# Norm sums by 32 columns of ones in four column groups, and norm roots held as rows of 128 tokens

## The reference

```python
def sandwich(x, mod, g_pre, g_post, fn):                 # first block: four times
    shift, scale, gate = mod
    h = rms_norm(x, g_pre) * (1.0 + scale[:, None]) + shift[:, None]
    return x + gate[:, None] * rms_norm(fn(h), g_post)

for i in range(DEPTH):                                   # second block: two layers
    m = hybrid_mixer(...) if i % 2 == 0 else mla_mixer(...)
    h = layer_norm(DN_ALPHA * x + m, ln1_g[i], ln1_b[i])
    f = jnp.square(jax.nn.relu(h @ mlp_w1[i])) @ mlp_w2[i]
    e = jax.nn.sigmoid(h @ ple_w_gate[i]) * (p[i] @ ple_w_proj[i])
    x = layer_norm(DN_ALPHA * h + f + e, ln2_g[i], ln2_b[i])
```

## Time and profile before

| | |
|---|---|
| median of three runs | 2917.77 us (2916.14 to 2920.08) |
| the profiled execution, whole time | 2916.7 us |
| its span from first to last instruction | 2914.9 us |
| PE, share of the span | 96% |
| PEld, share of the span | 80% |
| DVE, share of the span | 41% |
| POOL, share of the span | 32% |
| ACT, share of the span | 31% |

### The profile page before, as it was taken

One profiled execution on the slowest core, in us unless ns is written; L12 is line 12 of the kernel. 1 busy time (PEld: TensorE's weight loads), 2 busy tenths in 40 slices (PEclk: granted clock), 3 DMA queues, 4 the chain that ended last, 5 costly groups with the idle time before them and its releaser, 6 DMA issues.

```text
span 2914.9 us, 35811 instructions
## 1 busy us (share of the span) xinstructions
PE 2802.8 (96%) x14000; PEld 2325.7 (80%) x14000; DVE 1192.6 (41%) x1913; ACT 909.4 (31%) x1240; POOL 923.8 (32%) x223
## 2 busy tenths in 40 slices
PE   8998999999999999999999899999998999999998
PEld 7787888888778777888886787888887778788887
DVE  6666354053522234101248723614423561361532
ACT  3343322222333233222233524212223542421222
POOL 1220234433322222434333114444432111444431
PEclk9999999999999999999999999999999999999999
DMA  7430444343222211232222012222221111222221
GB/s 283 182 116 1 157 151 152 142 175 109 80 63 77 65 44 67 89 104 101 78 89 73 30 37 101 86 101 101 87 80 36 52 44 37 101 101 93 95 101 44
DMA packets 44457, 271.36 MB, mean 93 GB/s; under 512 B 5119, under 2 KB 8727, under 8 KB 16440
## 3 DMA queue, kind: packets, MB, share of 16 engines
q1 hardware_dynamic: 40320, 266.23, 25.6%
q10 hardware_dynamic: 4024, 3.54, 0.5%
HBM read 267.62 MB, written 2.13 MB: 93 GB/s over the span
## 4 chain that ended last, share of the span: by engine, by line
PE 66%; issue 25%; POOL 5%; DVE 3%; ACT 1%; POOLq 0%; DVEq 0%; ACTq 0%
PE lin L685 18%; PE lin L687 18%; PE lin L686 18%; POOL wlo L650 5%; PE bank L810 2%; PE bank L1115 1%; PE lin L1095 1%; PE bank L1107 1%; ACT whi L1556 1%; PE bank L1266 0%; PE bank L1383 0%; DVE dqr L2514 0%; PE bank L1247 0%; PE bank L1082 0%; PE bank L827 0%
## 5 line engine op out<-in xcount | busy, mean ns | idle before, releaser
L650 POOL TENSOR_TENSOR wlo<-raw,whi 128x2048 fp32r<-128x2048 f32 (+3 forms) x215 | 923.4, 4295 | 1950.4 <-ACT whi L1556 1950.4
L685 PE MATMUL lin<-hhi,whi 128*128 128x512 f32 x1976 | 786.2, 398 | 18.8 <-POOL wlo L650 8.6
L687 PE MATMUL lin<-hhi,wlo 128*128 128x512 f32 x1976 | 774.6, 392 | 0.0
L686 PE MATMUL lin<-hlo,whi 128*128 128x512 f32 x1976 | 774.5, 392 | 0.0
L1556 ACT ACTIVATE whi<-raw 128x2048 fp32r<-128x2048 f32 (+3 forms) x215 | 384.7, 1789 | 994.9 <-PE lin L687 955.5
L685 PEld LDWEIGHTS lin<-hhi,whi 128*128 128x128 f32 x1976 | 374.3, 189 | 110.1 <-issue 19.8
L685 PE MATMUL lin<-ghi,whi 128*128 128x512 f32 x1120 | 441.2, 394 | 0.8 <-issue 0.8
L687 PEld LDWEIGHTS lin<-hhi,wlo 128*128 128x128 f32 x1976 | 374.0, 189 | 79.7
L687 PE MATMUL lin<-ghi,wlo 128*128 128x512 f32 x1120 | 436.2, 389 | 0.0
L686 PE MATMUL lin<-glo,whi 128*128 128x512 f32 x1120 | 436.0, 389 | 0.0
L686 PEld LDWEIGHTS lin<-hlo,whi 128*128 128x128 f32 x1976 | 374.7, 190 | 76.3 <-issue 1.2
(11 more groups left out here) (407 smaller groups left out, 2807.2 us busy)
## 6 DMA issues: line engine op xcount, KB each, us to landing
raw<-in_w SPq DMA_DIRECT2D x169, 1024.0 KB, 4.9
adw_a<-in_ada SPq DMA_DIRECT2D x30, 1024.0 KB, 4.9
adw_b<-in_ada SPq DMA_DIRECT2D x18, 1024.0 KB, 5.0
raw<-in_w SPq DMA_DIRECT2D x20, 768.0 KB, 4.3
raw<-in_w SPq DMA_DIRECT2D x16, 640.0 KB, 3.8
raw<-in_w SPq DMA_DIRECT2D x10, 512.0 KB, 3.5
x<-in_x SPq DMA_DIRECT2D x1, 2048.0 KB, 16.9
out<-x SPq DMA_DIRECT2D x8, 256.0 KB, 2.0
```

What stands on the lines that cost most here:

```text
L650: nc.gpsimd.tensor_tensor(wlo[:, slot, 0:size], raw[:, slot, 0:size], whi[:, slot, 0:size].bitcast(F32), ALU.subtract).then_inc(s.wlo_ok, 1)
L685: pe.matmul(dst, lh, rh, start=first, stop=False)
L686: pe.matmul(dst, lh, rl, start=False, stop=False)
L687: return pe.matmul(dst, ll, rh, start=False, stop=last)
```

## The change

The sums are turned over. The stationary operand becomes 32 columns of ones, the moving one the 128x128 piece of the squares, and the result goes to 32 partitions: group t of the tokens to partitions 32t to 32t+31 of the first 128 columns of the bank, each row the same 128 sums. The four matmuls of a chunk so use four column groups of the array. Root and reciprocal are taken of the whole 128x128 block (`r_rows`), in place of 128x4. The spread takes a broadcast column of the identity as the stationary operand, which picks row 32t, and the 128x128 rows as the moving one. Between the sums `keep_busy` runs twice in place of once in `norm_sums`, `ada_sums_first` and `mla_mixer`. The head norms of the first mixer keep `column_sums` and `spread`.

```diff
+        r_rows = sb("r_rows", [P, P])
+        mu_rows, ms_rows, k_rows = tmp[:, 1, 0:P], tmp[:, 1, P:2 * P], tmp[:, 1, 0:P]
...
+            def chunk_sums(bank, src, first, last):
+
+                for t in range(TT):
+                    mm = pe.matmul(bank[32 * t:32 * t + 32, 0:P], ones[:, 0:32], src[:, t * P:(t + 1) * P],
+                                   start=first, stop=last)
+                return mm
...
-                column_sums(B4, sq[:, k % 2, :], k == 0, k == DC - 1).then_inc(s.ss_mm, 1)
+                chunk_sums(B4, sq[:, k % 2, :], k == 0, k == DC - 1).then_inc(s.ss_mm, 1)
...
+            def spread_rows(bank, rows):
+
+                for t in range(TT):
+                    mm = pe.matmul(bank[:, t * P:(t + 1) * P], ident[:, 32 * t:32 * t + 1].broadcast_to([P, P]), rows,
+                                   start=(t == 0), stop=(t == TT - 1))
+                return mm
...
-                spread(B7, r4).then_inc(s.rr_mm, 1)
+                spread_rows(B7, r_rows[:, :]).then_inc(s.rr_mm, 1)
...
-                    keep_busy(1 if c < DC - 1 else 0)
+                    keep_busy(2 if c < DC - 1 else 0)
...
-                            keep_busy(1, LB[3])
+                            keep_busy(2, LB[3])
...
-                    column_sums(B5, m[:, k, :], k == 0, k == DC - 1)
-                    column_sums(B4, sq[:, k % 2, :], k == 0, k == DC - 1).then_inc(s.ss_mm, 1)
+                    chunk_sums(B5, m[:, k, :], k == 0, k == DC - 1)
+                    chunk_sums(B4, sq[:, k % 2, :], k == 0, k == DC - 1).then_inc(s.ss_mm, 1)
...
-                    keep_busy(1, LB[0])
+                    keep_busy(2, LB[0])
...
-                act.activation(r4, sums_of(B4), ACT.Sqrt, bias=eps, scale=scale).then_inc(s.rms_ok, 1)
+                act.activation(r_rows[:, :], B4[:, 0:P], ACT.Sqrt, bias=eps, scale=scale).then_inc(s.rms_ok, 1)
...
-                act.activation(mu4, sums_of(B5), ACT.Copy, scale=1.0 / D).then_inc(s.mu_ok, 1)
-                act.activation(ms4, sums_of(B5), ACT.Square, scale=1.0 / D).then_inc(s.act_to_dve, 1)
+                act.activation(mu_rows, B5[:, 0:P], ACT.Copy, scale=1.0 / D).then_inc(s.mu_ok, 1)
+                act.activation(ms_rows, B5[:, 0:P], ACT.Square, scale=1.0 / D).then_inc(s.act_to_dve, 1)
...
-                v.reciprocal(r4, r4).then_inc(s.rr_ok, 1)
+                v.reciprocal(r_rows[:, :], r_rows[:, :]).then_inc(s.rr_ok, 1)
```

More of the change, by code:

```diff
@@ L245, in program @@
         minus_spl = small[:, 16:20]
-        mu4, ms4, k4, spare = small[:, 48:52], small[:, 52:56], small[:, 56:60], small[:, 60:61]
+        spare = small[:, 60:61]
         mmax = small[:, 20:24]
@@ L1310, in layer_sums @@
                     pe.wait_ge(s.sq_ok, n.up(s.sq_ok))
-                    column_sums(B5, m[:, k, :], k == 0, k == DC - 1)
-                    column_sums(B4, sq[:, k % 2, :], k == 0, k == DC - 1).then_inc(s.ss_mm, 1)
+                    chunk_sums(B5, m[:, k, :], k == 0, k == DC - 1)
+                    chunk_sums(B4, sq[:, k % 2, :], k == 0, k == DC - 1).then_inc(s.ss_mm, 1)
             def layer_rows():
                 pe.wait_ge(s.mu_ok, n.up(s.mu_ok))
-                spread(B6, mu4)
+                spread_rows(B6, mu_rows)
                 root_rows(5)
@@ L1410, in mla_mixer @@
                     pe.wait_ge(s.sq_ok, n.up(s.sq_ok))
-                    column_sums(B4 if c < 4 else B5, sq[:, c % 2, :], c in (0, 4), c in (3, 5)).then_inc(s.ss_mm, 1)
+                    chunk_sums(B4 if c < 4 else B5, sq[:, c % 2, :], c in (0, 4), c in (3, 5)).then_inc(s.ss_mm, 1)
                     if c == 0:
@@ L1418, in mla_mixer @@
                 pe.wait_ge(s.rr_ok, n.up(s.rr_ok))
-                spread(B5, k4).then_inc(s.rr_mm, 1)
+                spread_rows(B5, k_rows).then_inc(s.rr_mm, 1)
                 keep_busy(4, LB[0])
@@ L1902, in z_squares @@
                 tile[0] += DC
-                act.activation(mu4, sums_of(B5), ACT.Copy, scale=1.0 / D).then_inc(s.mu_ok, 1)
-                act.activation(ms4, sums_of(B5), ACT.Square, scale=1.0 / D).then_inc(s.act_to_dve, 1)
+                act.activation(mu_rows, B5[:, 0:P], ACT.Copy, scale=1.0 / D).then_inc(s.mu_ok, 1)
+                act.activation(ms_rows, B5[:, 0:P], ACT.Square, scale=1.0 / D).then_inc(s.act_to_dve, 1)
                 act.wait_ge(s.dve_to_act, n.up(s.dve_to_act))
-                act.activation(r4, r4, ACT.Sqrt, bias=eps_ln).then_inc(s.rms_ok, 1)
+                act.activation(r_rows[:, :], r_rows[:, :], ACT.Sqrt, bias=eps_ln).then_inc(s.rms_ok, 1)
                 split_next()
@@ L2018, in mla_mixer @@
                 act.wait_ge(s.ss_mm, n.up(s.ss_mm, 2))
-                act.activation(r4, sums_of(B4), ACT.Sqrt, bias=eps_rms, scale=1.0 / 512).then_inc(s.rms_ok, 1)
-                act.activation(k4, sums_of(B5), ACT.Sqrt, bias=eps_rms, scale=1.0 / 256).then_inc(s.rms_ok, 1)
+                act.activation(r_rows[:, :], B4[:, 0:P], ACT.Sqrt, bias=eps_rms, scale=1.0 / 512).then_inc(s.rms_ok, 1)
+                act.activation(k_rows, B5[:, 0:P], ACT.Sqrt, bias=eps_rms, scale=1.0 / 256).then_inc(s.rms_ok, 1)
                 for c in range(6):
@@ L2582, in layer_norm @@
                 v.wait_ge(s.act_to_dve, n.up(s.act_to_dve))
-                v.scalar_tensor_tensor(r4, sums_of(B4), 1.0 / D, ms4, ALU.mult, ALU.subtract).then_inc(s.dve_to_act, 1)
+                v.scalar_tensor_tensor(r_rows[:, :], B4[:, 0:P], 1.0 / D, ms_rows, ALU.mult, ALU.subtract).then_inc(s.dve_to_act, 1)
                 recip()
@@ L2710, in mla_mixer @@
                 skip(7)
-                for cols in (r4, k4):
+                for cols in (r_rows[:, :], k_rows):
                     v.wait_ge(s.rms_ok, n.up(s.rms_ok))
```

## The result

The changed kernel takes 2883.86 us, median of four runs (2882.36 to 2887.24), against 2917.35 (2916.14 to 2920.08) for the kernel before on the same chip: a ratio of 0.9885, interval 0.987 to 0.9899. It is faster by 33.5 us; 24.6 were forecast. The profiled execution took 2882.36 us, of which 2880.6 are its span.

The account below looks back on a forecast made before the run. PE, busy 96% of the span, was taken as the bound. Projections -31.2 us and norm ends +6.6 sum to -24.6: 2892.1 from the profiled 2916.7, 2893 against the median; range 2875 to 2922, for full overlap 2875 to 2900.

Parts of the forecast that it names:

- The sum: Inside projections, one chunk's sum falls from 0.89 to 0.62 us and two in a row from 1.79 to 0.84.
- the switch: Going from whole-array to part-array matmuls and back, at each block of sums: 0.40 us, with 0 as other bound.
- The block of three: Three sums together behind the first unit of the second mixer's projection; the third waits for ACT's square: 0.3 us saved.
- ln1's ends: End of ln1's projection, twice: the last sum gives PE back 1.2 us earlier each, 2.4 for two.
- The reciprocal and the root: On each norm's path, 128x128 in place of 128x4: reciprocal 0.95 us, 0.78 more; root 0.37, 0.1 more.
- The ends of the norms: Longer root and reciprocal less 0.5 given back: +0.4 us per first-block projection end, +1.0 per `norm_sums` with its slower pace.
- the last mixer: The last mixer's norms: five paces of 0.15 us and two reciprocals, partly beneath `keep_busy`, 0.9 lost.
- ln2's ends: Ends of ln2, two: shorter last sums save 1.3 us, the longer chain through the reciprocal takes most back: -0.1 each.
- The first pre norm: First norm of the kernel: eight sums at 1.48 in place of 1.32 us and a later, longer reciprocal: 1.3 lost.
- (A): Rival: column groups don't overlap; a sum costs 1.26 us, a pair 2.12, the kernel 2971, +53; chance 0.14.
- (B): Rival: column groups overlap in twos; a sum costs 0.83 us, a pair 1.26, the kernel about 2920; chance 0.12.
- (C): Rival: PE's longer waits at twelve norms lower the clock, up to 1.5 us each, 2905 to 2911; chance 0.08.

## Why the prediction was right

The likeliest case, all four groups at once, is what happened, and 2883.9 lies in its own range (2875 to 2900). The gain was 33.5 where 24.6 were forecast, so the mechanism was right and several terms were mis-sized, nearly all to the same side. By the prediction's own steps:

**The sum** was predicted at 0.62 and a pair at 0.84. They take 0.56 and 0.77. The streaming term, 0.22 per sum, was right; the mis-sized term is the switch, 0.40 taken from matmuls on half the rows and 0.34 measured. The trace of the kernel before had no nearer row. The 21 single sums so save 0.33 each, 6.9 us (5.7 predicted), the 24 pairs 1.02 each, 24.5 (22.8).

**The block of three** was put at 0.3, because the third sum waits for ACT. It gave 1.05: before, the three cost 2.80 us (from 1083.53 on the trace of before, where the 24 records stand together), after, 1.75 (1081.76 to 1083.51):

```profile
1081.53 0.39 PE L689 MATMUL lin<-ghi,wlo 128*128 128x512 f32 x1
1081.85 0.64 PE L818 MATMUL bank<-sq,cst 128*32 128x128 f32 x16
1083.05 0.43 PE L818 MATMUL bank<-sq,cst 128*32 128x128 f32 x8 [0.56 <-ACT sq L1639]
1083.40 0.50 PE L687 MATMUL lin<-ghi,whi 128*128 128x512 f32 x1
```

The wait is real (0.56), but the square that ends it (it starts at 1082.40, released by PE's sums) needs a buffer that the first sums free, and they free it earlier. The step that failed took ACT's square as fixed in time.

**ln1's ends** were right: from the start of the last square to the product 2.60 before, and after from 1735.92 to 1737.18 + 0.11, 1.37:

```profile
1735.92 0.63 ACT L1916 ACTIVATE sq<-m 128x512 f32<-128x512 f32 x1 [5.65 <-DVE m L2587]
```

```profile
1736.60 0.43 PE L818 MATMUL bank<-m,cst 128*32 128x128 f32 x8 [0.91 <-ACT sq L1916]
...
1737.18 0.50 PE L687 MATMUL lin<-ghi,whi 128*128 128x512 f32 x1
```

Twice 1.23, 2.5 us (2.4 predicted). The projections together: 6.9 + 24.5 + 1.1 + 2.5 = 35.0 us, against 31.2.

**The reciprocal and the root** were right to the row: 953 ns (0.95) and 368 ns (0.37).

**The ends of the norms** were put too dear, since the shorter last sum gives back more than the 0.5 taken. In `norm_sums` the last sum starts 1.52 ahead of the reciprocal in the earlier trace rows and 0.96 ahead of it now, though the root between them is 0.11 longer: 0.67 given back. From the last sum to the spread it is 1.97 after 1.75. The pace is 1.42 (1.48 predicted, 1.39 in the earlier trace rows), and from the first sum to the last it is 9.92 after 9.75. That is 0.22 + 0.17 = 0.4 for each `norm_sums` where 1.0 was predicted, 1.2 for the three in place of 3.0. The pace was put too high by the same switch as above. The four projection ends cost 0.17 each in place of 0.4, the last mixer 0.3 in place of 0.9.

**ln2's ends** were put at -0.1 each, and the spread comes 0.8 earlier at each. Before:

```profile
2895.08 0.63 ACT L1900 ACTIVATE sq<-m 128x512 f32<-128x512 f32 x1 [12.05 <-DVE m L2575]
...
2898.65 0.18 DVE L2153 RECIPROCAL small<-small 128x4 f32<-128x4 f32 x1 [0.36 <-ACT small L1906]
...
2899.07 0.60 PE L817 MATMUL lin<-cst 128*128 128x256 f32 x2
...
2899.50 0.72 PE L827 MATMUL bank<-cst,small 128*128 128x128 f32 x5
```

After:

```profile
2861.43 0.63 ACT L1916 ACTIVATE sq<-m 128x512 f32<-128x512 f32 x1 [11.08 <-DVE m L2591]
...
2864.06 0.95 DVE L2169 RECIPROCAL r_rows<-r_rows 128x128 f32<-128x128 f32 x1 [0.47 <-ACT r_rows L1922]
2864.15 0.60 PE L826 MATMUL lin<-cst 128*128 128x256 f32 x2
...
2865.07 1.16 PE L843 MATMUL bank<-r_rows,cst 128*128 128x128 f32 x8 [0.33 <-DVE r_rows L2169]
```

Before, the reciprocal was done at 2898.83 and the spread started 0.67 later, behind PE's own `keep_busy`. The prediction summed the chain of mean, variance, root and reciprocal as if it were the path, and did not see that PE was the late one. Now PE waits for the reciprocal and the longer 0.95 sits mostly in that slack: from square to spread 3.64 in place of 4.42.

At the other ln2 it is 3.66 in place of 4.43, but there the spread itself is slow. Before and after:

```profile
2175.88 1.05 PE L827 MATMUL bank<-cst,small 128*128 128x128 f32 x8
```

```profile
2155.59 2.05 PE L843 MATMUL bank<-r_rows,cst 128*128 128x128 f32 x8
```

The granted clock is 1.00 from 2172 to 2181 us before, and 0.72 from 2153 to 2159 us after. So the 0.8 is lost again: from the last product ahead of the last sums to the first one behind the norm it is 11.38 us in place of 11.15. The two ends together give 0.6, not 1.6.

**The first pre norm** was put at +1.3. PE's first product starts at 53.85 in place of 50.83, +3.0. Here the first sums run at half pace, and `keep_busy` is dear there. After:

```profile
31.22 0.66 PE L818 MATMUL bank<-sq,cst 128*32 128x128 f32 x8
31.81 2.08 PE L826 MATMUL lin<-cst 128*128 128x256 f32 x4
...
37.44 1.13 PE L826 MATMUL lin<-cst 128*128 128x256 f32 x4
```

Two rounds take 2.08 at first and 1.13 later, about twice as long. That this is the lower level of the clock is read from the pace alone: the profile gives the granted clock as 1.00 from 28 to 32 us, before the change and after. Before, all eight sums ran at the fast pace. When it comes differs between executions of one kernel: in the repeated run of the changed kernel sums already take 0.42 at 32.77, and the product starts at 52.37. In the run with paired sums, whose edit leaves this stretch alone, all eight sums are fast and it starts at 51.33. So only 0.5 of the 3.0 comes with the change where the pace is the same as before, less than the 1.3 predicted; the other 2.5 differs from execution to execution. The longer reciprocal is not on the path here at all: from the last sum to the next step for which PE waits (at 46.70 before and 50.21 after) it is 6.14 and 6.15.

**The sum.** -35.0, +0.7 at projection ends, +1.2 in `norm_sums`, +0.3 in the last mixer, -0.6 at ln2, +3.0 at the start make -30.4; the spans differ by -34.3. The 3.9 left over lie in stretches at the lower clock that the two executions have in different places. Both traces hold the same 9864 products; taken one by one, their distances away from the sums and norms add up to 3.5 us less after, nearly all of it in stretches with the lower clock in one trace alone, where the step is 0.43 us against 0.23. One such stretch is behind the first layer norm, before and after:

```profile
1745.00:1800.00 55.00, 52.10 (x246) 43.22 (x245) 20.82 (x31) 27.34 (x40) 20.79 (x5) 0.97 0.28 96
```

```profile
1745.00:1800.00 55.00, 52.09 (x230) 42.51 (x229) 19.31 (x28) 28.11 (x36) 23.78 (x6) 1.00 0.30 105
```

A clock of 0.97 over 55 us is 1.6 us. Why the two executions have these stretches at different places is open, and with one profile of each kernel this share of the gain can't be put down to the change. Against the -24.6 of the forecast the profiles differ by 9.7 more: 3.8 from the projections, 3.7 from the ends of the norms, 3.9 from such stretches, less 1.7 at the start, where the loss was greater than forecast.

**The rivals.** (A), no overlap, and (B), in twos, are ruled out: eight narrow records take 0.43 us in four groups and 1.06 in one, and the block costs 0.56, not the 0.83 of (B). (A) priced a sum without overlap at 1.26, against 1.19 in the run that made it so, and the kernel at 2971, against 2949.4 there with the first chunks still overlapping. (C), the clock at the norms, did not come in the mean: 0.987 to 0.990 in the four runs against 0.988. It came at one norm, the first ln2, as above; the repeated run has it there too (0.73 from 2153 to 2159 us), and so has the run with one `keep_busy` (0.72), the run with paired sums does not, and the one with the short reciprocal has it at the second ln2 in its place (0.72 from 2857 to 2863 us). Before its last pair of sums PE now idles for 1.64 us where it idled for 0.43, which fits (C)'s words that the sums keep it busy for less; but the second ln2 of the changed kernel idles as long and its spread runs at the full pace, so the cause is not shown. With one `keep_busy` the mean clock is 0.985 and 0.986. So the second `keep_busy` costs some 5 us on the path, and the times differ by 2.2; that the rest is clock which it buys is the likely reading, and not shown.

## What to carry to other kernels

When a matmul is there only to sum over partitions, the ones as a narrow stationary operand in four column groups let four f32 streams run at once over the same rows, as they did here. Count the blocks, not the sums: each block of narrow matmuls between whole-array ones pays 0.34 us once, so gather as many as the buffers allow before the switch; narrow matmuls that have no partner in another column group lose (1.19 against 0.89 for a sum). And what is spared on one engine is paid where the result is longer: 128 columns cost the reciprocal 0.77 us more than 4 did, in full at seven of the fourteen norms, in part at two and not at all at the other five.

## What the runs showed of the hardware

Matmuls in different column groups overlap fully though they use the same rows and different moving data: the narrow sum streams in 0.21 us, the time of one of its four groups. The prediction weighed the share in the Trainium skill, "TensorE: Matmul & The Clock Gate", Part 3, a speedup of 2.38 for three column groups; in these runs four groups give (1.19 - 0.34) / 0.21, 4.0, for the streaming alone, and 1.19 / 0.56, 2.1, with the switch counted. The same part's rule that a load overlaps running matmuls only where its row group differs does not hold here: eight loads that all use the same rows lie together in 0.16 us, while the matmuls of the first ones, 285 ns each, still run. At full width the eight loads take 1.09 us, also beside running matmuls.

The granted clock differs from one execution of the same kernel to the next by up to 0.003, and the times follow it: 2882.36 and 2882.75 at 0.989 and 0.990, 2887.24 at 0.987. Differences of a few us between two kernels here need that number beside them.
